# Turning the operands of a fp32 two-block layer by quarters of the TensorE array instead of by whole 128x128 transposes

## What is computed

```
x = x + sliding_window_attention(rms_norm(x, mixer_norm), positions, w_qkv, ..., w_o)
x = x + (silu(h @ w_gate) * (h @ w_up)) @ w_down            # h = rms_norm(x, ffn_norm)
...
ht = rmsnorm(mlstm_chunkwise(q, k, v, li, lf), g_head)       # 8 heads of 512
y = sigmoid(o) * ht * silu(z);   y @ a_w_out
...
y = band_attention(q, k, v, rel) * silu(z);   y @ b_w_out
x = x + gate * rmsnorm(y, g_post)
```

## Time and profile before

| | us |
|---|---|
| median of 3 runs | 2433.06 (2432.49 to 2433.09) |
| the profiled execution | 2432.94 |
| its span | 2431.2 |
| PE busy | 2414.9 (99%) |
| PE weight loads busy | 1974.1 (81%) |
| DVE busy | 1725.9 (71%) |
| ACT busy | 1169.4 (48%) |

### The profile page before, as it was taken

The page is one execution under the profiler, slowest core; times in us unless marked ns, Lnnn a source line. Parts: engine busy times, 40 slices in busy tenths (PEclk is TensorE's granted clock), DMA queues, the critical chain, the costliest instruction groups (busy, mean ns, idle before and its releaser), DMA issues.

```text
span 2431.2 us, 30291 instructions
## 1 busy us (share of the span) xinstructions
PE 2414.9 (99%) x11073; PEld 1974.1 (81%) x11073; DVE 1725.9 (71%) x2420; ACT 1169.4 (48%) x1581; POOL 45.2 (2%) x65
## 2 busy tenths in 40 slices
PE   9999999999999999999999999999999999999998
PEld 7777888888888888778888888888888778888887
DVE  8885777777777776667678667677676676666665
ACT  6665444444444444544444434444444564455553
POOL 1000000000000000000000000000000000000000
PEclk9999999999999999999999999999999999999999
DMA  8445888888888887567777787777777567776654
GB/s 297 141 131 164 264 294 292 302 296 293 286 294 293 291 294 238 157 223 239 238 233 233 243 261 240 242 230 239 234 235 240 157 192 255 241 238 209 233 191 138
DMA packets 161826, 578.11 MB, mean 238 GB/s; under 512 B 18288, under 2 KB 20592, under 8 KB 161680
## 3 DMA queue, kind: packets, MB, share of 16 engines
q1 hardware_dynamic: 160432, 572.64, 71.8%
q0 software_dynamic: 1104, 3.28, 0.5%
q10 hardware_dynamic: 144, 0.26, 0.0%
HBM read 574.01 MB, written 2.10 MB: 237 GB/s over the span
## 4 chain that ended last, share of the span: by engine, by line
PE 93%; DVE 3%; ACT 2%; issue 1%; DMA 1%; POOL 0%; SPq 0%; DVEq 0%; ACTq 0%
PE PS L1144 29%; PE PS L1146 29%; PE PS L1145 29%; PE PS L775 1%; DVE WL L2126 1%; ACT WH L1515 1%; DMA X<-in_x 0%; PE PS L875 0%; PE PS L848 0%; PE PS L863 0%; DVE X L2093 0%; PE PS L971 0%; DMA ZG<-in_crow 0%; PE PS L991 0%; PE PS L992 0%
## 5 line engine op out<-in xcount | busy, mean ns | idle before, releaser
L2126 DVE TENSOR_TENSOR WL<-W,WH 128x1024 fp32r<-128x1024 f32 x814 | 991.1, 1224 | 540.9 <-ACT WH L1515 538.1
L1515 ACT ACTIVATE WH<-W 128x1024 fp32r<-128x1024 f32 x814 | 856.9, 1059 | 917.1 <-PE PS L1146 908.1
L1144 PE MATMUL PS<-WH,XTH 128*128 128x512 f32 x2144 | 856.8, 400 | 2.8 <-DVE XTL L1644 1.2
L1146 PE MATMUL PS<-WH,XTL 128*128 128x512 f32 x2144 | 836.4, 390 | 0.0
L1145 PE MATMUL PS<-WL,XTH 128*128 128x512 f32 x2144 | 835.2, 390 | 0.0
L1144 PEld LDWEIGHTS PS<-WH,XTH 128*128 128x128 f32 x2144 | 402.7, 188 | 91.7 <-issue 11.3
L1146 PEld LDWEIGHTS PS<-WH,XTL 128*128 128x128 f32 x2144 | 402.4, 188 | 85.8
L1145 PEld LDWEIGHTS PS<-WL,XTH 128*128 128x128 f32 x2144 | 403.1, 188 | 83.1 <-issue 3.8
L1144 PE MATMUL PS<-WH,YTH 128*128 128x512 f32 x1120 | 441.8, 394 | 2.8 <-DVE WL L2126 2.3
L1146 PE MATMUL PS<-WH,YTL 128*128 128x512 f32 x1120 | 436.4, 390 | 0.0
L1145 PE MATMUL PS<-WL,YTH 128*128 128x512 f32 x1120 | 436.1, 389 | 0.0
(11 more groups left out here) (280 smaller groups left out, 1160.3 us busy)
## 6 DMA issues: line engine op xcount, KB each, us to landing
W<-in_vec SPq DMA_DIRECT2D x192, 512.0 KB, 4.5
W<-in_avoz SPq DMA_DIRECT2D x192, 512.0 KB, 4.5
W<-in_wg SPq DMA_DIRECT2D x88, 512.0 KB, 4.7
W<-in_wu SPq DMA_DIRECT2D x88, 512.0 KB, 4.7
W<-in_wd SPq DMA_DIRECT2D x88, 512.0 KB, 4.7
W<-in_gate SPq DMA_DIRECT2D x64, 512.0 KB, 4.5
W<-in_aqk SPq DMA_DIRECT2D x64, 512.0 KB, 4.5
W<-in_aout SPq DMA_DIRECT2D x64, 512.0 KB, 4.4
```

Source lines behind the costliest of these rows:

```text
L1144: e.matmul(p, x, WH[:, g % NH, j], start=first, stop=False)
L1146: i = e.matmul(p, y, WH[:, g % NH, j], start=False, stop=last)
L1515: e.activation(WH[:, n % NH], W[:, i % NW], ACT.Copy).then_inc(s_hi, 1)
L2126: e.tensor_tensor(l, src, h.bitcast(F32), ALU.subtract).then_inc(s_lo, 1)
```

## The change

Each of the 31 groups of eight transposes becomes 32 plain products with the identity, each of 64 rows (tokens) by 64 columns (features) of the array. Rows 0 to 63 of the tokens (a=0) go to one bank and rows 64 to 127 (a=1) to another, so a bank now holds half of the token rows of all four feature tiles, where it held all rows of two tiles. Both banks are taken together, and the 32 products stand in one piece, before the tick. 248 transposes go and 992 products come.

```
+            def turns_by_rows(banks, src):
+                for j in range(4):
+                    for t in range(2):
+                        for a, (b, full) in enumerate(banks):
+                            r = slice(64 * a, 64 * a + 64)
+                            for c in range(2):
+                                o = b[64 * c:64 * c + 64, 128 * j + 64 * t:128 * j + 64 * t + 64]
+                                f = 128 * j + 64 * c
+                                i = e.matmul(o, src[r, t, f:f + 64], ident[r, r], start=True, stop=True)
+                                if (j, t, c) == (3, 1, 1):
+                                    i.then_inc(full, 1)
...
-                for half in range(2):
-                    b, full = take(("mid", f, half))
-                    w.wait_ge(s_mid, 2 * f + 2)
-                    four_turns(b, lambda j, t: MID[:, t, 128 * (2 * half + j):128 * (2 * half + j) + 128], full)
-                    give(("mid", f, half), s_yt, ver + 2 * slot + half + 1)
+                banks = [take(("mid", f, a)) for a in range(2)]
+                w.wait_ge(s_mid, 2 * f + 2)
+                turns_by_rows(banks, MID)
+                for a in range(2):
+                    give(("mid", f, a), s_yt, ver + 2 * slot + a + 1)
                     yield
```

```
+    def fours(ver):
+        return lambda kt, t: ver + 2 * (kt // 4) + 2
...
-            def halves_T(key, kts, scale, done):
-                b = full(key)
-                for j, kt in enumerate(kts):
-                    i = e.activation(YTH[:, kt], b[:, 256 * j:256 * j + 256], ACT.Copy,
-                                     scale=1.0 if scale is None else scale(kt))
+            def halves_T(key, k0, scale):
+                b, a = full(key), key[2]
+                if scale is None:
+                    i = e.activation(half_rows(YTH, k0, 4, a), bank_rows(b, 0, 4), ACT.Copy)
+                else:
+                    for j in range(4):
+                        i = e.activation(half_rows(YTH, k0 + j, 1, a), bank_rows(b, j, 1), ACT.Copy,
+                                         scale=scale(k0 + j))
                 i.then_inc(s_yh, 1)
...
-                for j, kt in enumerate(kts):
-                    src, h = b[:, 256 * j:256 * j + 256], YTH[:, kt].bitcast(F32)
-                    if scale is None:
-                        i = e.tensor_tensor(YTL[:, kt], src, h, ALU.subtract)
+                if scale is None:
+                    i = e.tensor_tensor(half_rows(YTL, k0, 4, a), bank_rows(b, 0, 4),
+                                        half_rows(YTH, k0, 4, a).bitcast(F32), ALU.subtract)
...
-        yield from outproj("Y", pairs(YT_FFN[gi]), 2 * n, "down%d" % gi, split=norm_2 if gi == 2 else None)
+        yield from outproj("Y", fours(YT_FFN[gi]), 2 * n, "down%d" % gi, split=norm_2 if gi == 2 else None)
```

More of the change, by code:

```diff
@@ L459, in score @@
         if h % 4 == 3:
-            yield from outproj("Y", pairs(YT_MIX[h // 4]), 8, "aout%d" % (h // 4), split=norm_3 if h == 7 else None)
+            yield from outproj("Y", fours(YT_MIX[h // 4]), 8, "aout%d" % (h // 4), split=norm_3 if h == 7 else None)
             free = at["g"]
@@ L480, in score @@
         yield ("start", "gate_z", j) + last()
-    yield from outproj("Y", pairs(YT_BAND), 8, "bout", split=last_rows)
+    yield from outproj("Y", fours(YT_BAND), 8, "bout", split=last_rows)
 def attention_steps(qready, at):
@@ L1000, in mix @@
                 yield from ticks(7)
[L1001 to L1005, removed]
+                banks = [take(("mixT", h, a)) for a in range(2)]
+                w.wait_ge(s_mix, at("y1"))
+                turns_by_rows(banks, G1)
+                for a in range(2):
+                    give(("mixT", h, a), s_yt, YT_MIX[h // 4] + 2 * (h % 4) + a + 1)
                     yield
@@ L1010, in to_T @@
                 yield from ticks(4)
[L1011 to L1016, removed]
+                banks = [take((key, n, a)) for a in range(2)]
+                w.wait_ge(s_qc0, n + 1)
+                w.wait_ge(s_qc1, n + 1)
+                turns_by_rows(banks, QC)
+                for a in range(2):
+                    give((key, n, a), s_kq, 2 * n + a + 1)
                     yield
@@ L1071, in band @@
                 yield from ticks(4)
[L1072 to L1076, removed]
+                banks = [take(("bT", j, a)) for a in range(2)]
+                w.wait_ge(s_bo, 4 * j + 4)
+                turns_by_rows(banks, ZG)
+                for a in range(2):
+                    give(("bT", j, a), s_yt, YT_BAND + 2 * j + a + 1)
                     yield
@@ L1334, in ffn @@
                 for half in range(2):
-                    s = 4 * slot + 2 * half
                     w.wait_ge(s_unit, free)
-                    halves_T(("mid", f, half), (s, s + 1), None, None)
+                    halves_T(("mid", f, half), 4 * slot, None)
                     yield
@@ L1416, in to_T @@
                         w.wait_ge(*filled(("bs", 4 * (n - 5) + 3)))
-                    e.activation(dst[:, 2 * half:2 * half + 2].rearrange("p a k -> p (a k)"), b[:, :],
-                                 ACT.Copy).then_inc(s_kq, 1)
+                    e.activation(half_rows(dst, 0, 4, half), bank_rows(b, 0, 4), ACT.Copy).then_inc(s_kq, 1)
                     yield
@@ L1474, in band @@
                 for half in range(2):
-                    s = 4 * j + 2 * half
                     w.wait_ge(s_unit, free)
-                    halves_T(("bT", j, half), (s, s + 1), None, None)
+                    halves_T(("bT", j, half), 4 * j, None)
                     yield
@@ L1576, in vector_program, with lows_Y @@
             n_y = [0]
-            def lows_Y(key, kts, scale):
-                b = Tb[TB[key][0]]
+            def lows_Y(key, k0, scale):
+                b, a = Tb[TB[key][0]], key[2]
                 n_y[0] += 1
                 w.wait_ge(s_yh, n_y[0])
-                for j, kt in enumerate(kts):
-                    src, h = b[:, 256 * j:256 * j + 256], YTH[:, kt].bitcast(F32)
-                    if scale is None:
-                        i = e.tensor_tensor(YTL[:, kt], src, h, ALU.subtract)
-                    else:
-                        i = e.scalar_tensor_tensor(out=YTL[:, kt], in0=src, scalar=scale(kt), in1=h,
+                if scale is None:
+                    i = e.tensor_tensor(half_rows(YTL, k0, 4, a), bank_rows(b, 0, 4),
+                                        half_rows(YTH, k0, 4, a).bitcast(F32), ALU.subtract)
+                else:
+                    for j in range(4):
+                        i = e.scalar_tensor_tensor(out=half_rows(YTL, k0 + j, 1, a), in0=bank_rows(b, j, 1),
+                                                   scalar=scale(k0 + j),
+                                                   in1=half_rows(YTH, k0 + j, 1, a).bitcast(F32),
                                                    op0=ALU.mult, op1=ALU.subtract)
@@ L1853, in ffn @@
                 for half in range(2):
-                    s = 4 * slot + 2 * half
-                    lows_Y(("mid", f, half), (s, s + 1), None)
+                    lows_Y(("mid", f, half), 4 * slot, None)
                     yield
@@ L2052, in band @@
                 for half in range(2):
-                    s = 4 * j + 2 * half
-                    lows_Y(("bT", j, half), (s, s + 1), None)
+                    lows_Y(("bT", j, half), 4 * j, None)
                     yield
```

16 lines of the change are left out of this document (12 added, 4 removed).

## The result

| | us |
|---|---|
| before, median of 5 runs | 2433.03 (2432.49 to 2433.09) |
| after, median of 5 runs | 2443.46 (2442.97 to 2443.79) |
| ratio after to before | 1.0044, interval 1.0033 to 1.0055 |
| the profiled execution of after | 2442.97, its span 2441.2 (before 2432.94, 2431.2) |

The changed kernel is 0.44% slower. Forecast were 2444.2 us and a range of 2438 to 2475.

The account below looks back on a forecast made before the run. PE was taken as the bound, busy 2414.9 of 2431.2 us. New pieces +40.0 less removed transposes 28.7 gave +11.3 us on 2432.94, so 2444.2 us; range 2438 to 2475, chance 0.83.

Parts of the forecast that it names:

- What goes: Transposes removed from PE: 56 half groups at 0.465 us and three whole groups at 0.90, 28.7 us in all.
- What comes: 31 pieces of 32 two-pass products added on PE, 1.29 us a group, 40.0 us in all.
- five main steps: Main products on PE just behind each new piece, taken as 1.26 us, as read behind L848.
- four quarters at once: Within each new piece, four array quarters load and multiply side by side: 16 rounds of 0.058 us; chance 0.62.
- hardly anything is waited for: PE's waits: longest total 3.2 us, so time the TensorE stream takes in or gives up moves the end equally.
- The step of a transpose: Inside a half group, transposes start 0.109 us apart, said to be set by a load of 128 columns, some 106 ns.
- Handing over: Giving TensorE 128 instructions in 0.92 us, 7 ns each, was priced at nothing; a slower hand-over was a rival, chance 0.12.
- the rival of 12 ns an instruction: Hand-over to TensorE limits each piece: 1.54 us in place of 0.92, +19 us, 2463 us; chance 0.12 for 2450 to 2463.
- Strict order: Rival: products start only after all earlier ones, 2.0 us in place of 0.92 a piece, 2478 us; chance 0.07.
- two or one at a time: Rivals: only two quarters run together, 2473 us, chance 0.09; or only one, 2530 us, chance 0.02.
- ACT and DVE: More, smaller copies in `mix`: +0.87 us a half on ACT, +0.4 to 0.6 on DVE, covered by buffers; priced at nothing.
- `fours` and the earlier bank: Next projection waits for the whole group, leaving 3 us; second bank wanted 1.4 us earlier, at worst 7 us; priced nothing.

Follow-up runs that it names:

- joined form of before: Kernel before with both halves of each group in one piece of eight whole transposes, both banks taken together: 2431.20 us against 2432.68, ratio 0.9995.
- arrangement by quarters: Changed kernel with its 32 products reordered, all eight of one array quarter, then the next quarter's: 3.58 us a group, 2.26 more than after.
- one-pass form: Changed kernel with each group's 32 products replaced by 16 one-pass transposes of 64 rows by 128 columns: 2429.76 us against 2432.72, ratio 0.9989.

## Why the prediction was right, and where it was not

**What goes.** 56 halves measured 0.468 and three whole groups 0.902 us: 28.9 us. The prediction had 28.7.

**What comes.** Forecast 1.29 us a group, measured 1.316, so 40.8 in place of 40.0. Term by term: the way in 0.32 (0.32), first to last start 0.94 (0.92), the way out 0.15 (0.15), five main steps 1.27 (1.26). The choice on which it hung, four quarters at once, held. Net of what goes, 11.9 us of loss in place of 11.3.

**Of which 10.0 reached the end.** PE's stream shows where the rest was taken back, when the starts of the same main product in the two traces are set side by side: 0.33 us in the first 30 us, 0.74 at 445 us, 0.40 at 2235 us, 0.07 at 2331, and 0.03 in each of the eight mLSTM heads, 1.8 of the 1.9 us. At the first two it is a wait for WL, at the third one for `cols` from ACT. That third wait is gone in the joined form of before as well, so the joining takes it off and not the quarters. The kernel before, then after, at about 29 us, and before at 445 us:

```profile
29.65 0.47 PE L1144 MATMUL PS<-WH,XTH 128*128 128x512 f32 x1 [0.89 <-DVE WL L2126]
```

```profile
29.28 0.47 PE L1169 MATMUL PS<-WH,XTH 128*128 128x512 f32 x1 [0.66 <-DVE WL L2155]
```

```profile
444.96 0.47 PE L1144 MATMUL PS<-WH,YTH 128*128 128x512 f32 x1 [0.49 <-DVE WL L2126]
```

The first lies ahead of any touched group, so it is not the change's doing. The second is absent in after: PE comes later there, and WL is ready. The prediction took "hardly anything is waited for" as nothing; the 1.1 us at 445 and 2235 are that step's size. They offset the 0.6 by which the net price of the groups was forecast too low, and that the two errors have opposite signs is luck: without it the time would have come out 0.6 us above the forecast, still far inside the range.

**The step of a transpose.** "The step of a transpose is close to what a load of 128 columns takes" is the one step that did not hold. The number 0.109 was read from the timeline and held, so the sum was not touched. But the explanation rested on the load of a plain product (L848, 186 ns); a transposing load is listed with 140, and the moving columns are what costs (0.11 us with a load of only 8 columns, L934). Two causes with the same price, 0.107 for 128 columns of either, could not be told apart by their size; L934 stood in the trace of before and would have told. It had a cost: it hid that transposes of 64 rows, moving 64 columns, would halve the step.

**Handing over.** Priced at nothing, and right: 128 instructions go in within the 0.94 us, so the rival of 12 ns an instruction is out. Nor does 7 ns show as a limit: in the arrangement by quarters one quarter alone has the same step of 0.058 us.

**Strict order, two or one at a time.** Out by the windows: four starts in 0.02 us and rounds of 0.058. The arrangement by quarters shows what would have made the rival true, an order in which neighbours want the same quarter.

**ACT and DVE.** Price nothing, and right. In `mix` ACT's copies went from 13.4 to 18.5 us and DVE's from 14.0 to 18.0, 0.32 and 0.25 us a half where 0.87 and 0.4 to 0.6 were feared: an instruction over 128 elements took 384 and 343 ns, not 452 and 346 to 400. The unscaled copies and subtractions gave back 1.9 us on each engine (ACT 19.4 to 17.5, DVE 22.3 to 20.4), and both engines' totals moved by 0.5 us or less. No wait of PE grew.

**`fours` and the earlier bank.** Both priced at nothing; no wait of PE at either place in after, nor in the joined form of before.

## What to carry to other kernels

For fp32 pieces like these, price a piece on parts of the array as rounds times the longer of load and moving columns, plus about 0.38 us of PE for going in and out. With a fixed price of that size, the short pieces of this kernel gained only in the one-pass form, and little: more than half of what its groups saved came from joining the halves. Order the products so that neighbours go to different parts: the same 32 products cost 1.32 us in turn and 3.58 us part by part. And when two causes have the same price, look for a row in which only one of them is present before you name one.

## What was not expected of the hardware

- A transposing load of 128 fp32 columns costs about half of a plain one (listed 138 to 140 ns against 188; steps of 0.063 against 0.112 us with 64 rows), and the transposes' step follows their moving columns: 0.063 us at 64, 0.109 at 128, and still 0.11 at 128 when the load has only 8 columns.
- Row halves transpose side by side in fp32: 0.866 us a group against 0.894 for whole transposes, in spite of a fixed price of 0.36.
- A quarter of the array holds three or four passes that haven't started, and a full quarter blocks the others: 2.26 us a group when its eight products stand in a row.
- TensorE takes instructions of parts very fast: four quarters get their first load and product 7 ns apart, and 128 instructions go through in 0.94 us, 7 ns each, without showing as a limit: one quarter alone has the same step.
